# Where four small TensorE jobs stand in a chunked RWKV-7 solve: among the Gram products and the early levels, instead of between the turns of the later levels

## The chip, the core and the metric

The kernel runs on one core of a Trainium2 chip. The metric is the device time of one execution in microseconds (us). The kernel before took 1748.77 us, the median of 3 runs (1746.99 to 1751.68). The engines are called PE (TensorE, matrix products), ACT (ScalarE), DVE (VectorE), POOL (GpSimd) and SP (which only issues transfers).

## The reference, cut to what matters

Two encoder layers on 512 tokens of width 1024. The change lies in the first layer's RWKV-7 mixer, a linear recurrence over time, run forward and backward for 8 heads of width 64:

```
def rwkv7_step(state, inp):
    r, w, k, v, kk, a = inp
    sa = einsum('...vk,...k->...v', state, -kk)
    state = state * w[..., None, :] + sa[..., :, None] * (kk * a)[..., None, :] + v[..., :, None] * k[..., None, :]
    y = einsum('...vk,...k->...v', state, r)
    return state, y
...
decay = exp(-exp(w_log))          # w_log from a low-rank product of wl with w2
a = sigmoid(a0 + low-rank product of al with a2)
bonus = sum(rh[:, :, None] * kh * r_k, axis=(2, 4))
out = (y + bonus[..., None] * vh)
```

The rest (spatial gating, differential attention, cross-attention, gated feed-forward blocks) is not touched.

## The kernel before, in words

The recurrence is solved in chunks of 64 tokens: 8 chunks, 2 directions, and 4 pairs of heads (`j` = 0 to 3, two heads of 64 in 128 partitions). A pair is one call of `pair_pe`, `pair_act`, `pair_dve`, with some work of `pair_pool`. There is no scheduler: each engine runs a list of instructions in the order in which these functions write them, and waits on semaphores. What stands ahead of a waiting instruction on an engine is done, and what stands behind it waits too.

A pair on PE:

- `gram_pe` (L1197): 64x64 products of AR with BET (L1210, into banks 4 and 5 of PSUM), then four groups of 64x128 products (L1224): BET direction 0 into banks 6 and 7, BET direction 1 into banks 0 and 1, KAP direction 0 into 4 and 5, KAP direction 1 into 6 and 7. DVE masks them out of PSUM (`gram_dve`, L1691 to L1699, later `gram_k_dve`, L1705 and L1706).
- Five levels (`lv` = 0 to 4) that double the solved blocks of a triangular inverse. At level 0: products L1333, a mask on DVE (XX, L1745), products L1359, copies on ACT (UU, L1558). At levels 1 to 4: products L1337 for both directions, then the turn of UU for direction 0 (four transposes, L1317, into bank 4), a copy of it on ACT (TT, L1543), the turn for direction 1 into the same bank 4 (so it waits for that copy, `p_t0`), its copy, and the products L1363 in two groups, one for each direction; the second waits for the second copy.
- `side_pe(T, j, s)`, s = 0 to 9: other work put into the levels. An even s = 2 lv stands between the two turns of level lv; an odd s = 2 lv + 1 stands behind the second products of level lv. It holds the bonus product (L1270), the two low-rank halves for the next pair (`lora_pe`, L1193, half 0 and half 1), transposes of AR (s = 5), of BET (s = 6, L1301) and of KAP (s = 7), and the products AXT (s = 8). `side_act` holds ACT's part of each: BON (L1505), the tanh of a half (L1487, TMP), copies AXT, GB (L1522), KPD.
- Steps of the previous pair's chain over chunks (`chain_pe`, L1241 and L1246) stand behind each of the two sides.
- A tail (L1379 to L1419), then the next pair's Gram products.

In the last pair (`j` = 3) gate products (L1261) stand in the place of the low-rank halves; in the first pair turns of values (L1137) stand in the place of chain steps, and ACT also carries copies of another part (HIS, L1088).

A product of float32 operands is two passes in the trace, a transpose is one, so 32 products are x64 there.

Of the kernel before, what the change touches and what calls it, by code (L numbers as in the profile page):

```python
# [29 lines left out]
NT = SEQ // P  # L30
# [60 lines left out]
def build(nc, a, out):  # L91
    sems = {}

    def S(name):
        if name not in sems:
            sems[name] = nc.alloc_semaphore(name)
        return sems[name]
# [1092 lines left out]
    def lora_pe(e, j, which, b0):  # L1190
# [3 lines left out]
                          start=True, stop=True)  # L1194
        mm.then_inc(S("p_lora"), 1)

    def gram_pe(T, j):  # L1197
        e = T.e
        ar = AR[j % 2]
        e.wait_ge(S("p_fm"), j + 1)  # L1200
        e.wait_ge(S("p_bet"), j + 1)
        if j > 0:
            e.wait_ge(S("p_rfree"), j)
        else:
            e.wait_ge(S("sgu_s"), SGU_G)
        for d in range(2):
            for t in range(NT):
                for hh in range(2):
                    for x in range(2):
                        mm = e.matmul(PS[xs(x), 4 + hh, (d * NT + t) * CH:(d * NT + t) * CH + CH],  # L1210
                                      ar[half(hh), d, 0, chunk(t, x)], BET[half(hh), d, chunk(t, x)], start=True, stop=True)
        mm.then_inc(S("p_a"), 1)

        for l, d, b in ((BET, 0, 6), (BET, 1, 0), (KAP, 0, 4), (KAP, 1, 6)):
            if l is KAP:
                e.wait_ge(S("p_afree" if d == 0 else "p_bfree"), 2 * j + (2 if d == 0 else 1))
            elif j > 0:
                e.wait_ge(S("p_yfree" if d == 0 else "p_pfree"), j)
            elif d == 1:
                e.wait_ge(*at("zu", "ev", 4))  # L1220
            for t in range(NT):
                for hh in range(2):
                    for x in range(2):
                        mm = e.matmul(PS[xs(x), b + hh, t * P:t * P + P].rearrange("p (s k) -> p s k", s=2),  # L1224
                                      l[half(hh), d, chunk(t, x)], ar[half(hh), d, 0:2, chunk(t, x)], start=True, stop=True)
            mm.then_inc(S("p_g"), 1)
# [37 lines left out]
    def side_pe(T, j, s):  # L1264

        e = T.e
        if s == 2:
            e.wait_ge(S("p_gfree"), 2 * (j + 1))
            e.wait_ge(S("p_bonus"), j + 1)
            e.matmul(PS[:, 6, :], rk("bones"), TMP[1][:, 0, :], start=True, stop=True).then_inc(S("p_bonmm"), 1)  # L1270
        elif s == 3:
            e.wait_ge(S("p_bonfree"), j + 1)
            if j + 1 < NJ:
                lora_pe(e, j + 1, 0, 6)
            else:
                gates_pe(e, 0)
        elif s == 4:
            if j + 1 < NJ:
                e.wait_ge(S("p_lorafree"), 2 * j + 3)
                lora_pe(e, j + 1, 1, 6)  # L1280
            else:
                e.wait_ge(S("f_gg"), 2)
                e.wait_ge(S("f_bg"), 2)
                gates_pe(e, 2)
        elif s == 5:
            if j + 1 < NJ:
                e.wait_ge(S("p_lorafree"), 2 * j + 4)
            else:
                e.wait_ge(S("f_gg"), NJ)
                e.wait_ge(S("f_bg"), NJ)  # L1290
            for d in range(2):
                for t in range(NT):
                    for hh in range(2):
                        mm = e.transpose(PS[:, 6 + hh, (d * NT + t) * HD:(d * NT + t) * HD + HD],
                                         AR[j % 2][half(hh), d, 0, t * P:t * P + P], KC[half(hh), HD * hh:HD * hh + HD])
            mm.then_inc(S("p_tok"), 1)
        elif s in (6, 7):
            e.wait_ge(S("p_tokfree"), 3 * j + s - 5)
            for d in range(2):
                for t in range(NT):  # L1300
                    mm = e.transpose(PS[:, 6 + d, t * P:t * P + P], (BET, KAP)[s - 6][:, d, t * P:t * P + P], ident)  # L1301
            mm.then_inc(S("p_tok"), 1)
        elif s == 8:
            e.wait_ge(S("p_tokfree"), 3 * j + 3)
            if j == 0:
                e.wait_ge(S("rw0_vtk"), NT)
            for d in range(2):
                for u in range(8):
                    hh, t = divmod(u, NT)
                    for x in range(2):  # L1310
                        mm = e.matmul(PS[xs(x), 6 + d, u * CH:u * CH + CH], GKA[xs(x), d, u, :],
                                      VTK[xs(x), t, j * P + HD * hh:j * P + HD * hh + HD], start=True, stop=True)
                mm.then_inc(S("p_x0"), 1)
# [182 lines left out]

    def side_act(A, j, s):
        e = A.e
        if s == 1 and j + 1 == NJ:
            e.wait_ge(S("p_bonus"), NJ)  # L1500
            fin_square_act(e, 0)
            fin_square_act(e, 1)
        elif s == 2:
            e.wait_ge(S("p_bonmm"), j + 1)
            e.activation(BON[j][:, :], PS[:, 6, :], ACT.Copy).then_inc(S("p_bonfree"), 1)  # L1505
        elif s in (3, 4):
            if j + 1 < NJ:
                prep_tanh_act(e, j + 1, s - 3, 6)
            else:
                fin_gate_act(e, 2 * s - 6)  # L1510
                fin_gate_act(e, 2 * s - 5)
        elif s == 5:
            e.wait_ge(S("p_tok"), 3 * j + 1)
# [4 lines left out]
        elif s in (6, 7):  # L1518
            e.wait_ge(S("p_tok"), 3 * j + s - 4)
            for d in range(2):  # L1520
                if s == 6:
                    i = e.activation(units(GB[:, d, :, CH:P]), PS[:, 6 + d, :].rearrange("p (t b k) -> p b t k", b=2, k=HD),  # L1522
                                     ACT.Copy)
                else:
                    i = e.activation(KPD[:, d, :, :], PS[:, 6 + d, :].rearrange("p (t k) -> p t k", k=P), ACT.Copy)
            i.then_inc(S("p_tokfree"), 1)
            if s == 7 and j + 1 < NJ:
                prep_exp_act(e, j + 1)
            elif s == 7:
                e.wait_ge(S("p_bet"), NJ)  # L1530
                hi_part(A)
        elif s == 9 and j + 1 == NJ:
            e.wait_ge(S("c_yfree"), j * STEPS)
            fin_square_act(e, j - 1)
        elif s == 8:
            for d in range(2):
                e.wait_ge(S("p_x0"), 2 * j + d + 1)
                e.activation(AXT[:, d, :, HD:P], PS[:, 6 + d, :].rearrange("p (u k) -> p u k", k=HD), ACT.Copy)\
                    .then_inc(S("p_ax"), 1)

    def turn_u_act(e, j, lv, d):
        e.wait_ge(S(f"p_tn{d}"), j * (LV - 1) + lv)
        e.activation(TT[:, d, :, :], PS[:, 4, :].rearrange("p (u k) -> p u k", k=CH), ACT.Copy).then_inc(S(f"p_t{d}"), 1)  # L1543

    def pair_act(A, j):
        e = A.e
        for lv in range(LV):
            if lv > 0:
                turn_u_act(e, j, lv, 0)
# [235 lines left out]
    def fin_square_act(e, j):  # L1785
        e.activation(YSQ[j][:, :], YL[:, j, :], ACT.Square).then_inc(S("f_sq"), 1)
# [1082 lines left out]
```

## Time and profile before

| what | value |
|---|---|
| median of 3 runs | 1748.77 us |
| the profiled execution, own time | 1745.65 us |
| its span in the trace | 1743.9 us |
| PE busy | 1690.4 us (97%) |
| DVE, ACT, POOL busy | 1044.2, 815.2, 457.6 us |
| the four pairs: their first Gram products start at | 153.3, 197.8, 245.1, 290.9 us |

The profile's page gives the busy time of each engine, the chain of work that ended last, and groups of instructions by line. A busy PE is not a PE at its peak: ends of products are modelled, and one that waits for its turn inside the array counts as busy. In the chain, "issue" is time in which an engine waited for nothing that the profile shows. Brackets in a row of the timeline give the engine's idle time ahead of that row and what ended it.

### The profile page before, as it was taken

How to read it: one execution, taken by the hardware profiler on the slowest of the kernel's cores; microseconds unless marked ns; L12 is line 12 of the kernel's file. 1: busy time of each engine (PE TensorE's matmuls, PEld its weight loads, DVE VectorE, ACT ScalarE, POOL GpSimd, SP SyncE). 2: the span in 40 equal slices, each digit the busy share in tenths (PEclk: the TensorE clock that was granted, in tenths of full speed). 3: DMA queues.
4: the chain of work that ended last, by engine and by line, in shares of the span. 5: the costliest groups of instructions: out<-in, count | busy, mean ns of one | idle time of the engine just before them, and what ended most of it. 6: DMA issues, size and time to landing. Idle time of an engine off the chain costs nothing.

```text
span 1743.9 us, 29667 instructions
## 1 busy us (share of the span) xinstructions
PE 1690.4 (97%) x12773; PEld 1385.1 (79%) x12773; DVE 1044.2 (60%) x1308; ACT 815.2 (47%) x1237; POOL 457.6 (26%) x407
## 2 busy tenths in 40 slices
PE   7999899899999999999999999999999999999999
PEld 6878788778888787888887886668887788788887
DVE  5478677356343666766675455975434455685667
ACT  5254555536553433543355236865654343453344
POOL 2002322220100472245310220540010166114620
PEclk9999999999999999999999999999999999999999
DMA  7210000243222565365443222003431275356534
GB/s 255 85 48 2 4 5 6 73 169 123 95 97 73 202 233 181 126 245 183 163 169 108 97 75 71 1 2 121 145 108 41 94 264 196 132 195 239 196 102 155
DMA packets 116925, 212.70 MB, mean 122 GB/s; under 512 B 4247, under 2 KB 50938, under 8 KB 116794
## 3 DMA queue, kind: packets, MB, share of 16 engines
q1 hardware_dynamic: 103239, 159.59, 27.2%
q0 software_dynamic: 13264, 51.09, 8.2%
q8 instruction: 101, 1.65, 0.4%
q14 instruction: 30, 0.25, 0.0%
q10 hardware_dynamic: 291, 0.12, 0.0%
HBM read 185.62 MB, written 25.17 MB: 121 GB/s over the span
## 4 chain that ended last, share of the span: by engine, by line
PE 74%; DVE 11%; ACT 6%; issue 3%; POOL 3%; DMA 3%; SPq 0%; DVEq 0%; ACTq 0%; POOLq 0%
PE PS L431 50%; PE PS L538 10%; POOL DW L671 2%; DVE WLO L397 1%; ACT WHI L386 1%; PE PS L1929 1%; DVE SS L2237 1%; PE PS L1898 1%; DMA WRAW<-ab_w_in 1%; PE PS L937 1%; DMA diff_dn<-DW 1%; PE PS L1379 1%; DVE AT L2249 1%; DVE SQN L1013 1%; PE PS L2068 1%
## 5 line engine op out<-in xcount | busy, mean ns | idle before, releaser
L397 DVE TENSOR_TENSOR WLO<-WRAW,WHI 128x2048 fp32r<-128x2048 f32 (+1 forms) x106 | 249.1, 2361 | 296.0 <-ACT WHI L386 296.0
L431 PE MATMUL PS<-HIS,WHI 128*128 128x512 f32 x856 | 334.6, 391 | 4.8 <-DVE LOS L2412 2.1
L431 PE MATMUL PS<-LOS,WHI 128*128 128x512 f32 x856 | 333.1, 389 | 0.0
L431 PE MATMUL PS<-HIS,WLO 128*128 128x512 f32 x856 | 333.1, 389 | 0.0
L386 ACT ACTIVATE WHI<-WRAW 128x2048 fp32r<-128x2048 f32 (+1 forms) x107 | 203.0, 1907 | 229.0 <-PE PS L431 181.6
L431 PE MATMUL PS<-WHI,HIS 128*128 128x512 f32 x608 | 240.4, 395 | 1.1 <-DVE LOS L728 1.1
L431 PE MATMUL PS<-WLO,HIS 128*128 128x512 f32 x608 | 236.9, 390 | 0.0
L431 PE MATMUL PS<-WHI,LOS 128*128 128x512 f32 x608 | 236.7, 389 | 0.0
L431 PEld LDWEIGHTS PS<-HIS,WHI 128*128 128x128 f32 x856 | 160.7, 188 | 42.4 <-issue 5.7
L431 PEld LDWEIGHTS PS<-HIS,WLO 128*128 128x128 f32 x856 | 160.7, 188 | 33.5
L431 PEld LDWEIGHTS PS<-LOS,WHI 128*128 128x128 f32 x856 | 160.7, 188 | 32.9
L431 PEld LDWEIGHTS PS<-WHI,HIS 128*128 128x128 f32 x608 | 114.2, 188 | 26.3 <-issue 1.8
L431 PEld LDWEIGHTS PS<-WLO,HIS 128*128 128x128 f32 x608 | 114.1, 188 | 24.3
L431 PEld LDWEIGHTS PS<-WHI,LOS 128*128 128x128 f32 x608 | 114.2, 188 | 22.9 <-issue 0.2
L538 PE MATMUL PS<-WHI,SHI 128*128 128x512 f32 x308 | 120.1, 390 | 0.8 <-DVE SLO L554 0.8
L538 PE MATMUL PS<-WLO,SHI 128*128 128x512 f32 x308 | 119.8, 389 | 0.0
L538 PE MATMUL PS<-WHI,SLO 128*128 128x512 f32 x308 | 119.8, 389 | 0.0
L394 DVE TENSOR_TENSOR WLO<-PW,WHI 128x1536 fp32r<-128x1536 f32 (+1 forms) x56 | 92.4, 1650 | 26.1 <-ACT WHI L382 25.9
L382 ACT ACTIVATE WHI<-PW 128x1536 fp32r<-128x1536 f32 (+1 forms) x56 | 76.8, 1378 | 64.2 <-PE PS L538 54.8
L671 POOL TENSOR_TENSOR DW<-RW 128x512 f32<-128x512 f32 x44 | 88.6, 2031 | 61.8 <-DMA diff_dn<-DW 46.1
L2024 ACT ACTIVATE SHI<-GX 128x256 fp32r<-128x256 f32 x44 | 18.4, 418 | 149.9 <-POOL GX L624 94.7
L746 POOL TENSOR_TENSOR SM<-SM 128x1 f32<-128x1 f32 x16 | 12.2, 797 | 244.8 <-DVE SM L754 236.4
(327 smaller groups left out, 2844.3 us busy)
## 6 DMA issues: line engine op xcount, KB each, us to landing
WRAW<-ffn_w_up SPq DMA_DIRECT2D x88, 512.0 KB, 4.9
RW<-ffn_w_down POOLq DMA_DIRECT2D x22, 1024.0 KB, 7.3
diff_dn<-DW POOLq DMA_DIRECT2D x22, 1024.0 KB, 5.3
WRAW<-cross_wkv SPq DMA_DIRECT2D x16, 1024.0 KB, 5.0
PW<-diff_dn SPq DMA_DIRECT2D x8, 1536.0 KB, 9.3
WRAW<-diff_w_in SPq DMA_DIRECT2D x12, 1024.0 KB, 5.1
WRAW<-ab_w_in SPq DMA_DIRECT2D x10, 1024.0 KB, 5.7
PW<-diff_dn SPq DMA_DIRECT2D x8, 1280.0 KB, 7.5
```

The lines of the kernel that those rows point to most:

```text
L382: A.e.activation(WHI[place(i)][:, 0:a1 - a0, :], PW[PW_PLACE[q]][:, a0:a1, :], ACT.Copy)\
L386: A.e.activation(part(WHI[place(i)], i), part(WRAW[raw_slot[i]], i), ACT.Copy).then_inc(S("w_hi"), 1)
L394: V.e.tensor_tensor(WLO[place(i)][:, 0:a1 - a0, :], PW[PW_PLACE[q]][:, a0:a1, :], WHI[place(i)][:, 0:a1 - a0, :].bitcast(F32), ALU.subtrac ...
L397: V.e.tensor_tensor(part(WLO[place(i)], i), part(WRAW[raw_slot[i]], i), part(WHI[place(i)], i).bitcast(F32), ALU.subtract).then_inc(S("w_l ...
L431: mm = e.matmul(o, l, r, start=(si == 0 and kk == 0 and q == 0), stop=(si == len(steps) - 1 and kk == nk - 1 and q == 2))
L538: mm = e.matmul(PS[:, bank + t, :], ht[part_of][:, m, t * P:t * P + P], wt[place(i)][:, m - a0, :], start=(fresh and m == 0 and r == 0), s ...
L671: e.tensor_tensor(DW[:, to, :], x, y, ALU.subtract).then_inc(sem(name, "wdif"), 1)
L937: mm = e.transpose(PS[:, bank0 + k % 4, t * P:t * P + P], tok[:, t, k * P:k * P + P], ident)
L1013: V.mine(e.reciprocal(SQN[j][:, :], SQN[j][:, :]))
L1379: mm = e.matmul(PS[xs(x), 2 * d + u // 4, (u % 4) * P:(u % 4) * P + P], UU[xs(x), d, u, :], AXT[xs(x), d, u, :], start=True, stop=True)
L1898: mm = e.matmul(PS[:, 4 * (t % 2) + h // 2, (h % 2) * MEM:(h % 2) * MEM + MEM], QFT[:, 2 * h + k, t * P:t * P + P], KFT[:, 2 * h + k, :], ...
L2024: A.e.activation(SHI[b - 2][:, gi, :], GX[:, (0, 4)[b - 2], gi, :], ACT.Copy).then_inc(sem(name, "hi"), 1)
```

## The change

Four jobs are moved; none is added or taken away.

- BET's transposes leave s = 6 (between the turns of level 3) and stand between BET's two groups of Gram products, in banks 2 and 3. ACT's copy of them (GB) is a new `gram_act`, ahead of level 0.
- The next pair's low-rank half 0 leaves s = 3 and stands between KAP's two groups of Gram products, in banks 2 and 3, behind that copy. Its tanh follows the copy in `gram_act`.
- The bonus product leaves s = 2 (between the turns of level 1) and stands behind level 0 (s = 1), in bank 3.
- The low-rank half 1 leaves s = 4 (between the turns of level 2) and stands at s = 3, where half 0 stood.

```
+    def tokens_pe(e, l, b0):
+        for d in range(2):
+            for t in range(NT):
+                mm = e.transpose(PS[:, b0 + d, t * P:t * P + P], l[:, d, t * P:t * P + P], ident)
+        mm.then_inc(S("p_tok"), 1)
...
         for l, d, b in ((BET, 0, 6), (BET, 1, 0), (KAP, 0, 4), (KAP, 1, 6)):
+            if l is BET and d == 1:
+                if j > 0:
+                    e.wait_ge(S("p_qfree"), j)
+                else:
+                    e.wait_ge(*at("zu", "ev", 4))
+                tokens_pe(e, BET, 2)
+            if l is KAP and d == 1 and j + 1 < NJ:
+                e.wait_ge(S("p_tokfree"), 3 * j + 1)
+                lora_pe(e, j + 1, 0, 2)
...
-        if s == 2:
+        if s == 1:
+            e.wait_ge(S("p_bonus"), j + 1)
+            e.matmul(PS[:, 3, :], rk("bones"), TMP[1][:, 0, :], start=True, stop=True).then_inc(S("p_bonmm"), 1)
+        elif s == 3:
             e.wait_ge(S("p_gfree"), 2 * (j + 1))
...
             if j + 1 < NJ:
-                lora_pe(e, j + 1, 0, 6)
+                lora_pe(e, j + 1, 1, 6)
...
-                if lv == 0 and d == 1 and j > 0:
-                    e.wait_ge(S("p_qfree"), j)
+                if lv == 1 and d == 1:
+                    e.wait_ge(S("p_bonfree"), j + 1)
+                if lv == 0 and d == 1:
+                    if j + 1 < NJ:
+                        e.wait_ge(S("p_lorafree"), 2 * j + 3)
+                    else:
+                        e.wait_ge(S("p_tokfree"), 3 * j + 1)
...
+    def gram_act(e, j):
+        e.wait_ge(S("p_tok"), 3 * j + 1)
+        for d in range(2):
+            i = e.activation(units(GB[:, d, :, CH:P]), PS[:, 2 + d, :].rearrange("p (t b k) -> p b t k", b=2, k=HD), ACT.Copy)
+        i.then_inc(S("p_tokfree"), 1)
+        if j + 1 < NJ:
+            prep_tanh_act(e, j + 1, 0, 2)
+
     def pair_act(A, j):
         e = A.e
+        gram_act(e, j)
```

PE's list at the Gram products of pair 1, before (AR_118 is this pair's AR, U_98 is U0; the brackets name the semaphores waited for):

```order
L1224 MATMUL PS<-AR_118,BET 64x128 [waits p_yfree]
L1224 MATMUL PS<-AR_118,BET 64x128 x15
L1224 MATMUL PS<-AR_118,BET 64x128 [waits p_pfree]
L1224 MATMUL PS<-AR_118,BET 64x128 x15
L1224 MATMUL PS<-AR_118,KAP 64x128 [waits p_afree]
L1224 MATMUL PS<-AR_118,KAP 64x128 x15
L1224 MATMUL PS<-AR_118,KAP 64x128 [waits p_bfree]
L1224 MATMUL PS<-AR_118,KAP 64x128 x15
L1333 MATMUL PS<-U_98,AI 64x64 [waits p_bfree,p_u0]
```

And the same place now (L1237 are the products of L1224, L1344 those of L1333; KC holds the identity):

```order
L1237 MATMUL PS<-AR_118,BET 64x128 [waits p_yfree]
L1237 MATMUL PS<-AR_118,BET 64x128 x15
L1200 MATMUL PS<-KC,BET 128x128 [waits p_qfree]
L1200 MATMUL PS<-KC,BET 128x128 x7
L1237 MATMUL PS<-AR_118,BET 64x128 [waits p_pfree]
L1237 MATMUL PS<-AR_118,BET 64x128 x15
L1237 MATMUL PS<-AR_118,KAP 64x128 [waits p_afree]
L1237 MATMUL PS<-AR_118,KAP 64x128 x15
L1193 MATMUL PS<-ZS_88,WL_73 128x512 [waits p_tokfree]
L1193 MATMUL PS<-ZS_88,WL_73 128x512
L1237 MATMUL PS<-AR_118,KAP 64x128 [waits p_bfree]
L1237 MATMUL PS<-AR_118,KAP 64x128 x15
```

Eight transposes and two low-rank products now stand inside the Gram products, and the first of the low-rank products waits for ACT's copy of the transposes.

ACT's list at levels 2 and 3 of pair 1, before (TMP_114 is the tanh of half 1, UU the copies behind L1363):

```order
L1543 ACTIVATE TT<-PS 128x512 [waits p_tn0]
L1487 ACTIVATE TMP_114<-PS,SM 128x512 [waits p_lora,p_bonmm,p_fm]
L1487 ACTIVATE TMP_114<-PS,SM 128x512
L1543 ACTIVATE TT<-PS 128x512 [waits p_tn1]
L1561 ACTIVATE UU<-PS 128x2x4x64 [waits p_un0]
L1561 ACTIVATE UU<-PS 128x2x4x64 [waits p_un1]
L1515 ACTIVATE AXT<-PS 128x8x64 [waits p_tok]
L1515 ACTIVATE AXT<-PS 128x8x64
L1543 ACTIVATE TT<-PS 128x512 [waits p_tn0]
L1522 ACTIVATE GB<-PS 128x8x64 [waits p_tok]
L1522 ACTIVATE GB<-PS 128x8x64
L1543 ACTIVATE TT<-PS 128x512 [waits p_tn1]
```

And the same place now (L1549 are the copies of L1543, L1576 those of L1561):

```order
L1549 ACTIVATE TT<-PS 128x512 [waits p_tn0]
L1549 ACTIVATE TT<-PS 128x512 [waits p_tn1]
L1576 ACTIVATE UU<-PS 128x2x4x64 [waits p_un0]
L1576 ACTIVATE UU<-PS 128x2x4x64 [waits p_un1]
L1525 ACTIVATE AXT<-PS 128x8x64 [waits p_tok]
L1525 ACTIVATE AXT<-PS 128x8x64
L1549 ACTIVATE TT<-PS 128x512 [waits p_tn0]
L1549 ACTIVATE TT<-PS 128x512 [waits p_tn1]
```

The two copies of a level's turns now follow each other with nothing between them, at level 2 and at level 3.

## Rows read from the trace of the kernel before

**Rows 1.** Busy time over the four pairs (length, then each engine's us and instructions)

```profile
150.00:340.00 190.00, 173.28 (x5630) 150.62 (x5628) 130.30 (x204) 99.57 (x164) 50.65 (x38) 1.00 0.07 21
```

**Rows 2.** Chain of waits, Gram stages of pairs 1, 2, 3 (start us, us, what)

```profile
198.27 1.80 issue
...
203.31 0.49 issue
...
211.15 0.52 issue
...
243.62 1.36 issue
...
247.97 0.84 issue
...
292.06 0.83 PE PS L1224 x30
292.89 1.37 issue
```

**Rows 3.** DMA queues from 150 to 340 us (packets, MB, share of 16 engines)

```profile
q8 instruction: 44, 0.72, 1.6%
```

**Rows 4.** Chain of waits, the moved kinds of work between other products

```profile
214.94 1.06 PE PS L1193 x4
...
228.01 1.04 PE PS L1301 x8
...
306.50 1.91 PE PS L1261 x4
```

**Rows 5.** Timeline of PE in pair 2 (start us, us, engine, line)

```profile
248.99 2.01 PE L1224 MATMUL PS<-AR,KAP 64*64 64x128 f32 x63
250.76 2.14 PE L1333 MATMUL PS<-U,AI 64*64 64x64 f32 x64
252.71 2.13 PE L1359 MATMUL PS<-XX,TT 64*64 64x64 f32 x64
254.88 0.45 PE L1241 MATMUL PS<-QT,PT 64*64 64x64 f32 x8
...
256.68 0.66 PE L1317 MATMUL PS<-KC,UU 128*128 128x128 f32 x4
...
258.03 0.65 PE L1317 MATMUL PS<-KC,UU 128*128 128x128 f32 x4
...
260.16 1.13 PE L1193 MATMUL PS<-ZS,WL 64*128 64x512 f32 x4
...
262.76 0.65 PE L1317 MATMUL PS<-KC,UU 128*128 128x128 f32 x4
...
264.41 0.66 PE L1317 MATMUL PS<-KC,UU 128*128 128x128 f32 x4
...
267.13 0.71 PE L1294 MATMUL PS<-KC,AR 64*128 64x64 f32 x16
...
270.08 0.66 PE L1317 MATMUL PS<-KC,UU 128*128 128x128 f32 x4
...
271.44 0.64 PE L1317 MATMUL PS<-KC,UU 128*128 128x128 f32 x4
...
273.99 1.09 PE L1301 MATMUL PS<-KC,KAP 128*128 128x128 f32 x8
```

**Rows 6.** Timeline of ACT in pair 2

```profile
253.90 0.60 ACT L1558 ACTIVATE UU<-PS 128x512 f32<-128x512 f32 x1 [7.45 <-PE PS L1359]
...
257.37 0.60 ACT L1543 ACTIVATE TT<-PS 128x512 f32<-128x512 f32 x1 [1.89 <-PE PS L1317]
...
264.60 1.26 ACT L1487 ACTIVATE TMP<-PS,SM 128x512 f32<-128x512 f32 x2 [0.56 <-PE PS L1193]
...
271.64 1.09 ACT L1522 ACTIVATE GB<-PS 128x512 f32<-128x512 f32 x2 [0.28 <-PE PS L1301]
```

**Rows 7.** Timeline of PE in pair 0

```profile
158.40 2.08 PE L1333 MATMUL PS<-U,AI 64*64 64x64 f32 x64 [0.20 <-DVE GB L1696]
```

More of the change, by code:

```diff
@@ L1266, in side_pe @@
         e = T.e
-        if s == 2:
+        if s == 1:
+            e.wait_ge(S("p_bonus"), j + 1)
+            e.matmul(PS[:, 3, :], rk("bones"), TMP[1][:, 0, :], start=True, stop=True).then_inc(S("p_bonmm"), 1)
+        elif s == 3:
             e.wait_ge(S("p_gfree"), 2 * (j + 1))
[L1269 to L1272, printed above, removed]
             if j + 1 < NJ:
-                lora_pe(e, j + 1, 0, 6)
+                lora_pe(e, j + 1, 1, 6)
             else:
@@ L1277, in side_pe @@
         elif s == 4:
[L1278 to L1281, printed above, removed]
+            if j + 1 == NJ:
                 e.wait_ge(S("f_gg"), 2)
@@ L1296, in side_pe @@
             mm.then_inc(S("p_tok"), 1)
[L1297 to L1302, printed above, removed]
+        elif s == 7:
+            e.wait_ge(S("p_tokfree"), 3 * j + 2)
+            tokens_pe(e, KAP, 6)
         elif s == 8:
@@ L1498, in side_act @@
         e = A.e
[L1499 to L1503, printed above, removed]
+        if s == 1:
             e.wait_ge(S("p_bonmm"), j + 1)
-            e.activation(BON[j][:, :], PS[:, 6, :], ACT.Copy).then_inc(S("p_bonfree"), 1)
+            e.activation(BON[j][:, :], PS[:, 3, :], ACT.Copy).then_inc(S("p_bonfree"), 1)
+            if j + 1 == NJ:
+                fin_square_act(e, 0)
+                fin_square_act(e, 1)
         elif s in (3, 4):
-            if j + 1 < NJ:
-                prep_tanh_act(e, j + 1, s - 3, 6)
-            else:
+            if s == 3 and j + 1 < NJ:
+                prep_tanh_act(e, j + 1, 1, 6)
+            elif j + 1 == NJ:
                 fin_gate_act(e, 2 * s - 6)
@@ L1512, in side_act @@
         elif s == 5:
-            e.wait_ge(S("p_tok"), 3 * j + 1)
+            e.wait_ge(S("p_tok"), 3 * j + 2)
             for d in range(2):
@@ L1517, in side_act @@
             i.then_inc(S("p_tokfree"), 1)
-        elif s in (6, 7):
-            e.wait_ge(S("p_tok"), 3 * j + s - 4)
+        elif s == 7:
+            e.wait_ge(S("p_tok"), 3 * j + 3)
             for d in range(2):
[L1521 to L1525, printed above, removed]
+                i = e.activation(KPD[:, d, :, :], PS[:, 6 + d, :].rearrange("p (t k) -> p t k", k=P), ACT.Copy)
             i.then_inc(S("p_tokfree"), 1)
-            if s == 7 and j + 1 < NJ:
+            if j + 1 < NJ:
                 prep_exp_act(e, j + 1)
-            elif s == 7:
+            else:
                 e.wait_ge(S("p_bet"), NJ)
@@ L1543, in turn_u_act @@
         e.activation(TT[:, d, :, :], PS[:, 4, :].rearrange("p (u k) -> p u k", k=CH), ACT.Copy).then_inc(S(f"p_t{d}"), 1)
+    def gram_act(e, j):
[3 more added lines that the diff above has]
+        i.then_inc(S("p_tokfree"), 1)
+        if j + 1 < NJ:
+            prep_tanh_act(e, j + 1, 0, 2)
     def pair_act(A, j):
         e = A.e
+        gram_act(e, j)
         for lv in range(LV):
```

2 lines of the change are left out of this document (removed).

## The prediction

> **What bounds the kernel now.** I read the windows of the four pairs first, then the chain of waits through them, then the timelines of PE and ACT at the places that the change touches. In the windows the reader is to see that PE is busy for 173.28 of 190.00 us [rows 1]: no other engine is near that, so the stage ends when PE's list ends, and an edit is worth what it does to the time between two starts on PE. The other engines matter only where PE waits for them.
>
> In the chain the reader is to see two kinds of wait. One is "issue", time for which the profile names no other engine: six such gaps, 0.49 to 1.80 us long, at or near the Gram products of pairs 1 to 3 [rows 2]. In the same 190 us the instruction queue moved 44 packets while PE ran 5630 passes [rows 1, 3], which is one packet for 128 passes (a weight load and a product each). So I take the gaps for waits for code: a block of 128 passes can't start before its packet has come, and short products (L1333: 64 passes from 250.76 to 252.71, 30 ns each [rows 5]) run through a block in less than the 4.3 us that a packet took on average (190.00 by 44). The other kind is ACT's copy TT between and behind the two turns of a level.
>
> In the timeline of PE the distances from start to start tell what a place costs. At level 1 the second turn starts 1.35 us after the first (256.68 to 258.03), and that is the copy and not the bonus product between them: ACT's TT runs from 257.37 to 257.97 [rows 5, 6]. At level 2 the distance is 1.65 (262.76 to 264.41), set by the low-rank half; at level 3 it is 1.36 (270.08 to 271.44), the copy again.
>
> **The change part by part.** Terms are taken for a pair, start to start on PE, and then added over the pairs. Positive is slower.
>
> *What the Gram stage and level 0 gain in work.* The eight transposes cost 1.04 between 64x64 products, the low-rank half 1.06, and the bonus product 0.95 (half of the 1.91 of the two gate products, which are of the same shape and stand between the same kinds of work) [rows 4]. Together 3.05 in pairs 0 to 2. Pair 3 has no low-rank half: 1.99.
>
> *What hides it there.* Where PE runs without a wait, L1333 starts 0.24 before the modelled end of L1224 (250.76 against 248.99 + 2.01 = 251.00) [rows 5]; so each gap that the views show is 0.24 longer from start to start. In pair 1 the transposes fall into the block that ends in the 0.49 gap, among KAP's groups, which gives back 0.73; the 0.52 gap at 211.15 stands behind all three jobs and gives back 0.76 [rows 2]. In pair 2 the 0.84 gap (1.08) comes between BET and KAP, which runs from 248.99, so it stands behind the transposes and gives them back whole; the chain step at 254.88 waited for the mask GKR behind L1359's end at 254.84 (0.04, so 0.28), which the bonus product now covers [rows 2, 5]. The gaps at 198.27 and 243.62 stand ahead of the moved work and stay. In pair 3 the 1.37 gap at 292.89 comes after 30 of the 32 passes of BET's first group, so just ahead of the transposes, and gives nothing back [rows 2]. In pair 0 there is no gap of this kind, but L1333 waited 0.20 for DVE (0.44) [rows 7], and GKR held the next step as in pair 2, 0.28. For pair 3 I take the same two, 0.72.
>
> Left over: pair 0, 3.05 - 0.72 = 2.33. Pair 1, 3.05 - 1.49 = 1.56. Pair 2, 3.05 - 1.36 = 1.69. Pair 3, 1.99 - 0.72 = 1.27.
>
> *What the levels give back.* Level 1: nothing. The bonus product stood in the 1.35 that the copy takes in any case, and half 1 takes the place of half 0 behind it. Level 2: the second turn comes at 1.35 instead of 1.65, 0.30. From the second turn to the next work behind both groups of L1363 it takes 2.13 at level 1 (258.03 to 260.16), where nothing waits, and 2.72 at level 2 (264.41 to 267.13), where ACT's tanh (264.60, 1.26) stands ahead of the second copy: 0.59. Level 3: 0.01 between the turns, and 2.55 (271.44 to 273.99) against 2.13 behind them, where GB's copy (1.09) stood in the way: 0.42 [rows 5, 6]. So 1.32 in pairs 1 and 2. Pair 3 keeps its gate products between the turns of level 2 and gains level 3 alone, 0.43. In pair 0 ACT also carries the HIS copies in these levels, which the change does not move; bounds 0 and 1.32, and I take half, 0.66, since neither is nearer.
>
> *New waits.* The transposes wait for QT's copies, which ACT makes while PE runs L1210; the half waits for GB's copy, 1.09 on an ACT that stood idle for 7.45 there [rows 6], and BET's second and KAP's first group stand between (32 passes each; 63 took 2.01 [rows 5]), so I count nothing. If ACT were late, KAP's second group and all behind it would be late by as much. L1333's second group waits for the tanh, 1.26 on ACT against 32 passes of KAP and 32 of L1333. L1337's second group at level 1 waits for BON's copy, with a chain step and the first group ahead of it. POOL's L1650 writes BET for the next pair and waits for the transposes; it can only start earlier, and the next pair's L1210 needs it much later, so I count nothing. No transfer is moved.
>
> *The sum.* Pair 0: 2.33 - 0.66 = 1.67. Pair 1: 1.56 - 1.32 = 0.24. Pair 2: 1.69 - 1.32 = 0.37. Pair 3: 1.27 - 0.43 = 0.84. Together 3.1 us slower: 1745.65 + 3.1 = 1748.8 by the profiled execution. That execution lies 3.1 below the median of the runs, so the forecast of a median is 1748.77 + 3.1 = 1751.9, 0.18% more. I call anything within 0.3% (5.2 us) no change, which is about what a measurement of this kernel can tell.
>
> **The rivals.**
>
> *The levels don't give it back (slower).* The place is XX's mask on DVE at level 3 and the code block that ends there: if the second group of L1363 then waits for one of these instead of for ACT's copy, the 0.66 + 1.32 + 1.32 + 0.43 = 3.73 of the levels go, and the sum is 6.8: 1755.6. It decides for "slower" once less than 1.6 of the 3.73 comes. For it: DVE has its scans at level 2, just ahead of that mask. Against it: the rows name ACT, not DVE, at both places, and ACT's obstacle is gone.
>
> *The gaps don't fill (slower).* If the "issue" gaps are not bound to the count of passes, work put ahead of them only pushes them back: 0.73 + 0.76 + 1.08 = 2.6 more, 5.7 in all, 1754.4. For it: the profile names no releaser there. Against it: the packets and the 128 passes. The Trainium skill, "Runtime: NRT & Kernel Launch", section "Instruction fetch mechanics", says that a queue of the sequencer's own fills a buffer of 2048 instructions for this engine in blocks of 256, and that the cost of crossing a block is mostly hidden; by that the gaps would have another cause and this rival would hold. The trace agrees with the blocks (44 packets for 5630 passes of two instructions) and not with the hiding.
>
> *All of it hides (no change, a little faster).* If the moved work costs nothing in the Gram stage, because DVE's masks or the code set its pace from end to end, only the 3.73 remains: 1745.0. For it: six gaps there. Against it: three of them stand ahead of the moved work.
>
> *It also lets the code run ahead (faster).* If slow passes in a block let later packets come early, the 1.80 and 1.36 gaps at 198.27 and 243.62 go as well: 1741.9. Against it: a whole tail of short products stands between the moved work and the next pair's Gram products.
>
> **How the numbers follow.** Forecast 0.50; levels don't give back 0.18; gaps don't fill 0.12; all hides 0.14; code runs ahead 0.06. So slower 0.30, same 0.64 (0.50 + 0.14), faster 0.06. The forecast's own bounds: the three jobs' prices by a tenth each way (0.3 in a pair, 1.1 in all), pair 0's levels by 0.66 each way, pair 3's two small waits by 0.72 upwards: 1751.9 less 1.8 and more 2.5. The range reaches over both slower cases and leaves out the two below: 1747.5 to 1756.5.
>
> **What would show it.** In the profile after, at pair 2: the first and second turns of levels 2 and 3 both 1.35 apart; the second group of L1363 there no longer behind ACT; no "issue" gap between the transposes and L1333's successor in pairs 1 and 2, but those at the tail's end and ahead of the transposes unchanged; the chain step of level 1 later by some 1.5 to 2.3 us from the pair's start, and level 4 by less than half of that. Wrong would be the forecast if the Gram stage got no longer, or if the wait at level 3 came back under another engine's name. By this the span would be near 1747.0 (1743.9 + 3.1); one under 1743 or over 1752 would show the size wrong.

## The result: slower by 0.4%, near the upper end of the range

| | median of the runs | runs | against before |
|---|---|---|---|
| before | 1749.36 us (1744.34 to 1751.68) | 6 | |
| after | 1755.41 us (1752.93 to 1759.53) | 6 | 1.0042, 95% interval 1.0024 to 1.006 |

The medians lie 6.0 us apart where 3.1 were forecast: inside the range of 1747.5 to 1756.5, but slower, not "no change". The page of the kernel after, its busy times:

```profile
PE 1698.3 (97%) x12773; PEld 1390.6 (79%) x12773; DVE 1046.0 (60%) x1308; ACT 816.8 (46%) x1237; POOL 458.2 (26%) x407
```

DVE, ACT and POOL are busy within 1.8 us of before; PE is busy 7.9 us longer. Part of that is the clock: the profiled execution (own time 1759.53, span 1757.7) ran at a mean granted clock of 0.996, that of before at 1.000. Windows of after (length, busy us of PE, PEld, DVE, ACT, POOL with instructions, granted clock, DMA share, GB/s):

```profile
150.00:340.00 190.00, 170.23 (x5316) 146.02 (x5316) 127.45 (x198) 97.99 (x161) 48.47 (x36) 0.98 0.06 17
...
190.00:194.00 4.00, 4.00 (x70) 4.00 (x66) 4.00 (x9) 0.87 (x3) 0.21 (x1) 0.58 0.02 4
194.00:251.00 57.00, 49.59 (x1738) 43.53 (x1734) 37.73 (x60) 26.00 (x41) 15.56 (x13) 1.00 0.02 4
251.00:255.00 4.00, 3.97 (x105) 3.64 (x106) 1.62 (x3) 1.09 (x2) 1.72 (x2) 0.57 0.01 4
255.00:340.00 85.00, 77.62 (x2443) 66.15 (x2442) 54.32 (x92) 44.81 (x74) 18.72 (x14) 1.00 0.11 33
```

In the same 190 us PE gets through 5316 passes, not 5630, and is idle 19.8 us, not 16.7 [rows 1]. Two short stretches stand at 0.58 and 0.57, that is mostly at 1.2 GHz instead of 2.4. (More such time lies behind the pairs: from 356 to 360 us the clock is 0.65.) What follows compares starts on PE stage by stage, so that these stretches can be told from the rest.

The chain of waits, its "issue" gaps at the Gram stages after (start us, us, what):

```profile
201.38 1.80 issue
...
249.12 1.91 issue
```

The gaps of 0.49, 0.52 and 0.84 [rows 2] are gone, and those ahead of the moved work stay, as forecast (1.80 is 1.80 again, 1.36 is 1.91 in this execution). At level 3 of pair 1 the chain before ran over ACT's GB copy:

```profile
225.60 1.08 ACT GB L1522 x2
226.68 0.50 ACT TT L1543
```

After, it runs over a scan on DVE:

```profile
226.19 1.23 DVE TMP L1609
227.41 3.23 DVE TMP L1610
230.64 0.18 DVE QT L1267
230.82 0.21 DVE YL L1270
231.03 0.04 issue
231.07 0.45 PE PS L1254 x8
```

Two engines' timelines show why (L1609 and L1610 are the two scans of the next pair's decay, L1665 is POOL's product of the rate and KK into the next pair's BET, L1303 AR's transposes, L1323 a turn, L1254 the chain step behind it, L1200 KAP's transposes; brackets: idle time ahead and what ended it):

```profile
222.41 1.05 POOL L1660 TENSOR_SCALAR TMP<-TMP 128x1024 f32<-128x1024 f32 x1 [6.08 <-ACT TMP L1498]
226.77 2.79 POOL L1665 TENSOR_TENSOR BET<-KK,TMP 128x1024 f32<-128x1024 f32 x1 [3.32 <-PE PS L1303]
...
226.19 1.23 DVE L1609 TENSOR_TENSOR_SCAN TMP<-RC,TMP 128x512 f32<-128x512 f32 x1
227.33 3.31 DVE L1610 TENSOR_TENSOR_SCAN TMP<-RC,TMP 128x512 f32<-128x512 f32 x1
...
277.12 3.32 DVE L1610 TENSOR_TENSOR_SCAN TMP<-RC,TMP 128x512 f32<-128x512 f32 x1
...
223.74 0.66 PE L1323 MATMUL PS<-KC,UU 128*128 128x128 f32 x4 [0.69 <-ACT TT L1549]
...
225.88 0.71 PE L1303 MATMUL PS<-KC,AR 64*128 64x64 f32 x16
...
229.41 0.66 PE L1323 MATMUL PS<-KC,UU 128*128 128x128 f32 x4 [0.69 <-ACT TT L1549]
231.07 0.45 PE L1254 MATMUL PS<-QT,PT 64*64 64x64 f32 x8 [1.01 <-DVE YL L1270]
...
232.90 1.09 PE L1200 MATMUL PS<-KC,KAP 128*128 128x128 f32 x8
```

The second scan takes 3.31 us where the first takes 1.23. It ends at 230.64, 1.08 after POOL's product (226.77 + 2.79 = 229.56): it has waited for POOL and then run. The chain step on PE waits for DVE's steps behind that scan. Second turn to KAP's transposes is 3.49 (229.41 to 232.90) where 2.13 was forecast. Pair 2's scan at 277.12 takes as long, and the same distance is 2.90 there. In the kernel before the scans were over when POOL began:

```profile
222.31 1.23 DVE L1594 TENSOR_TENSOR_SCAN TMP<-RC,TMP 128x512 f32<-128x512 f32 x1
223.45 1.20 DVE L1595 TENSOR_TENSOR_SCAN TMP<-RC,TMP 128x512 f32<-128x512 f32 x1
...
227.09 1.56 DVE L1606 TENSOR_SCALAR TMP<-TMP,COLS,SM 128x1024 f32<-128x1024 f32 x1
...
225.74 2.37 POOL L1650 TENSOR_TENSOR BET<-KK,TMP 128x1024 f32<-128x1024 f32 x1 [4.01 <-PE PS L1301]
```

There it lay over another DVE instruction, the scaling L1606, which takes 1.56 under it (0.81 after, at L1621, where POOL stands idle), and the chain above does not run over that.

The reason is a line that the diff does not touch. POOL's product waits for the second of the pair's three signals `p_tok`. Before, the second was BET's transposes, at level 3; now BET's come first, and the second is AR's, at the end of level 2. So the product starts earlier in its pair, 25.91 us behind pair 1's Gram start (226.77 less 200.86) where it was 27.99 before (225.74 less 197.75). Before, it came 1.09 after the end of the second scan; now it comes 0.56 ahead of that scan's start. Its operand is ready at 223.46 (222.41 + 1.05): released by BET's own signal it could run ahead of both scans.

### The profile page after: what moved, and what is told of

Read it like the earlier page. It is cut to its first block, busy times and chain, and to the rows that moved or that the text cites. A ratio compares the mean times of both kernels' runs of the same rounds, so it can differ in the third digit from the quotient of the medians.

```text
span 1757.7 us, 29668 instructions
## 1 busy us (share of the span) xinstructions
PE 1698.3 (97%) x12773; PEld 1390.6 (79%) x12773; DVE 1046.0 (60%) x1308; ACT 816.8 (46%) x1237; POOL 458.2 (26%) x407
## 4 chain that ended last, share of the span: by engine, by line
PE 74%; DVE 11%; ACT 6%; issue 3%; POOL 3%; DMA 3%; SPq 0%; DVEq 0%; ACTq 0%; POOLq 0%
PE PS L431 49%; PE PS L538 10%; POOL DW L671 2%; DVE WLO L397 1%; ACT WHI L386 1%; PE PS L1944 1%; DVE SS L2252 1%; PE PS L1913 1%; DMA WRAW<-ab_w_in 1%; PE PS L937 1%; PE PS L1237 1%; PE PS L1390 1%; DMA diff_dn<-DW 1%; DVE AT L2264 1%; DVE SQN L1013 1%
## 5 line engine op out<-in xcount | busy, mean ns | idle before, releaser
L431 PE MATMUL PS<-HIS,WHI 128*128 128x512 f32 x856 | 334.5, 391 | 4.5 <-DVE LOS L2427 1.5
L431 PE MATMUL PS<-HIS,WLO 128*128 128x512 f32 x856 | 333.2, 389 | 0.0
L431 PE MATMUL PS<-LOS,WHI 128*128 128x512 f32 x856 | 333.1, 389 | 0.0
L431 PE MATMUL PS<-WHI,HIS 128*128 128x512 f32 x608 | 241.5, 397 | 1.1 <-DVE LOS L728 1.1
L431 PE MATMUL PS<-WHI,LOS 128*128 128x512 f32 x608 | 237.6, 391 | 0.0
L431 PE MATMUL PS<-WLO,HIS 128*128 128x512 f32 x608 | 237.6, 391 | 0.0
L431 PEld LDWEIGHTS PS<-HIS,WHI 128*128 128x128 f32 x856 | 160.7, 188 | 42.6 <-issue 3.6
L431 PEld LDWEIGHTS PS<-HIS,WLO 128*128 128x128 f32 x856 | 160.7, 188 | 33.7
L431 PEld LDWEIGHTS PS<-LOS,WHI 128*128 128x128 f32 x856 | 160.7, 188 | 32.5
L431 PEld LDWEIGHTS PS<-WHI,HIS 128*128 128x128 f32 x608 | 114.8, 189 | 26.5 <-issue 1.8
L431 PEld LDWEIGHTS PS<-WLO,HIS 128*128 128x128 f32 x608 | 114.7, 189 | 24.4
L431 PEld LDWEIGHTS PS<-WHI,LOS 128*128 128x128 f32 x608 | 114.8, 189 | 23.2 <-issue 0.2
```

The lines of the kernel that those rows point to most:

```text
L431: mm = e.matmul(o, l, r, start=(si == 0 and kk == 0 and q == 0), stop=(si == len(steps) - 1 and kk == nk - 1 and q == 2))
```

## The bill by stages

Starts on PE, after less before, and the forecast's terms sorted into the same stages (the 0.52 gap of pair 1 lay 13.4 us behind its Gram start, so in the second row). "Early" is the first experiment below. Each column is one profiled execution.

| stage | forecast | after | early |
|---|---|---|---|
| Gram start to L1333's products: pairs 0, 1, 2, 3 | 1.66, 1.37, 1.02, 0.60 | 1.75, 1.75, 2.79, 0.70 | 1.75, 1.48, 1.22, 0.98 |
| to level 1's second turn | 0.67, 0.19, 0.67, 0.67 | 0.75, 0.05, 0.59, 0.89 | 0.75, 0.05, 0.59, 0.89 |
| to level 3's first turn | -0.45, -0.89, -0.89, 0 | -0.40, -0.87, -1.06, 0 | -0.39, -0.88, -0.90, 0 |
| to the tail | -0.21, -0.43, -0.43, -0.43 | 0.10, 0.91, 0.33, -0.44 | -0.10, -0.35, -0.44, -0.44 |
| sum to the tails | 3.1 | 7.8 | 4.2 |
| tail to the next Gram start | 0 | 1.15, 1.10, -0.20 | 1.32, 0.28, 0.07 |

Two stages of after are off. Level 3 of pairs 1 and 2 costs 1.34 and 0.76 more than forecast: the scan. Pair 2's Gram stage costs 1.57 more than in "early", and it holds the stretch at half clock that starts behind 251; pair 0's tail holds the other. Pair 1's tail is 1.10 longer, of which 0.55 is the gap of 1.36 that is 1.91 here.

Such gaps differ from one execution to another with PE's list unchanged. In "before, with two copies split" below, where nothing is moved on PE, the 0.49, 0.52 and 0.84 are 0.20, 0.14 and 0.56. A difference of half a microsecond in one stage of one profile can be that alone.

## The experiments

The mean granted clock differs a little from run to run, and the last column takes that out: the time of each run less that of the kernel before at the same clock, from the runs of before that were measured with it (1.23 us for each 0.001 of clock, a line through 70 runs of the kernel before in three sets); mean and standard error. For the kernel after, whose line is that of all 70, it is +7.5; the three sets differ by up to 1.4 us at equal clock, so this figure is the least sure. The column is not what a run takes: if a kernel brings on a low clock itself, that cost is left out of it. The medians have it in.

| kernel | median us | ratio to before, 95% | at equal clock, us |
|---|---|---|---|
| product early | 1753.27 | 1.0032 (1.0020 to 1.0043) | +5.0, 0.3 |
| product late | 1754.24 | 1.0038 (1.0023 to 1.0052) | +5.1, 0.4 |
| bonus back | 1753.18 | 1.0034 (1.0021 to 1.0048) | +4.2, 0.3 |
| BET's transposes back | 1751.77 | 1.0021 (1.0008 to 1.0033) | +3.6, 0.5 |
| early, and bonus back | 1751.27 | 1.0012 (1.0000 to 1.0025) | +1.9, 0.3 |
| BET's transposes alone, product early | 1752.62 | 1.0027 (1.0014 to 1.0040) | +3.4, 0.5 |
| the same, product late | 1748.11 | 1.0017 (1.0001 to 1.0033) | +0.9, 0.4 |
| low-rank halves alone | 1746.75 | 0.9992 (0.9982 to 1.0002) | +0.1, 0.2 |
| before, with two copies split | 1747.67 | 0.9986 (0.9975 to 0.9996) | -3.0, 0.5 |
| low-rank halves, GB's copy split | 1747.39 | 1.0000 (0.9986 to 1.0014) | 0.0, 0.4 |

**POOL's product off the scan, early.** The kernel after, with the wait set to BET's own signal:

```diff
-            e.wait_ge(S("p_tok"), 3 * j - 1)
+            e.wait_ge(S("p_tok"), 3 * j - 2)
             e.tensor_tensor(BET[:, :, :], both(KK[:, j, :]), TMP[1][:, :, :], ALU.mult).then_inc(S("p_bk"), 1)
```

> The changed kernel, with POOL's product of KK and the rate (it writes the next pair's BET) waiting for the first p_tok signal of the pair, BET's transposes, instead of the second, which is AR's transposes in the new order. Theory A, collision: in the changed kernel this product (226.77 to 229.56) lies over DVE's second scan, which takes 3.31 instead of 1.2 us, and level 3's mask comes late. Then here the scans take 1.2 each in pairs 1 and 2, the distance from the second turn of level 3 to KAP's transposes falls from 3.5 (pair 1) and 2.9 (pair 2) to about 2.1, and the time falls by 1.5 to 2.2: a ratio to before near 1.003. Theory B, the clock alone (four stretches at half clock in the changed kernel's profile): the ratio stays near 1.004 whenever such stretches are there, and the level keeps its distances. Theory C, the Gram stage's terms alone: nothing changes.

Its timeline at level 3 of pair 1:

```profile
223.03 2.37 POOL L1665 TENSOR_TENSOR BET<-KK,TMP 128x1024 f32<-128x1024 f32 x1
...
225.97 1.23 DVE L1609 TENSOR_TENSOR_SCAN TMP<-RC,TMP 128x512 f32<-128x512 f32 x1
227.12 1.20 DVE L1610 TENSOR_TENSOR_SCAN TMP<-RC,TMP 128x512 f32<-128x512 f32 x1
...
228.90 0.66 PE L1323 MATMUL PS<-KC,UU 128*128 128x128 f32 x4 [0.69 <-ACT TT L1549]
...
231.03 1.09 PE L1200 MATMUL PS<-KC,KAP 128*128 128x128 f32 x8
```

The scan is back at 1.20 and the step at 2.13 (228.90 to 231.03), the forecast's number. The time falls by 2.1 from median to median, or 2.5 at equal clock. Against the runs of before that go with each, the medians give less, 6.0 down to 5.1, and the two ratios' intervals overlap; two more pairs of kernels below differ by this overlap, and at equal clock by 2.3 and 2.5. The rows are as theory A said. Early's profile has a stretch at half clock too (0.58, shown below), and level 3 is short all the same, so the clock alone (theory B) is not what lengthened it.

**The same from the other side, late.** `3 * j - 1` becomes `3 * j`, KAP's signal.

> The changed kernel, with POOL's product for the next pair's BET held back until KAP's transposes are done (third signal of the pair, not the second). Theory (what costs is that POOL's product lies over DVE's second scan): the scan at level 3 takes 1.2 us again, as it does when the product starts early, and the step from level 3's second turn to KAP's transposes is back near 2.1 us, in pairs 1 and 2 alike; the product then lies under DVE's scaling of the next pair's rows instead; time 1752.5 to 1754.5. Rival (the product must come early; what hurts is its lateness, not the overlap): pairs 1 and 2 stay as long as in the changed kernel or get longer, 1755 or more.

```profile
225.62 1.23 DVE L1609 TENSOR_TENSOR_SCAN TMP<-RC,TMP 128x512 f32<-128x512 f32 x1
226.77 1.20 DVE L1610 TENSOR_TENSOR_SCAN TMP<-RC,TMP 128x512 f32<-128x512 f32 x1
...
232.25 2.62 POOL L1665 TENSOR_TENSOR BET<-KK,TMP 128x1024 f32<-128x1024 f32 x1 [9.36 <-PE PS L1200]
...
228.85 0.66 PE L1323 MATMUL PS<-KC,UU 128*128 128x128 f32 x4 [0.69 <-ACT TT L1549]
...
230.98 1.09 PE L1200 MATMUL PS<-KC,KAP 128*128 128x128 f32 x8
```

5.5 us later than POOL had it, and again 1.20 and 2.13. So it is the overlap and not the lateness. The product lies beside other DVE instructions here. The masks among them, which read PSUM, take as long as elsewhere (XX, two in 1.29); an instruction on SBUF operands at its end, L1637, takes 1.17 for 0.68, and the step above is not longer for it. The medians alone would not tell this kernel from the one after; the rows and the equal-clock column do.

**The bonus product back** between level 1's turns (`if s == 1:` to `if s == 2:`, bank 3 to 6, with its waits), and this together with the early product:

> The changed kernel with the bonus product back between the turns of level 1. By the sum of the prediction the bonus cost 0.95 less 0.28 behind level 0 in each pair and nothing between the turns: 2.7 us less than the changed kernel, a ratio to before near 1.0025. Collision theory: the same, and level 3 stays as long as in the changed kernel. Rival, the bonus product was hidden behind level 0 by the mask GKR: no difference, ratio 1.004.

> The changed kernel, with POOL's product released early and the bonus product back between the turns of level 1. Theory: the two add, since the one lies at level 3 and the other at level 0: the early product takes away what it did alone (2 to 2.6 us) and the bonus what it did alone (1.3 to 3.5), which leaves +0.5 to +3 over the kernel before, with the same-clock runs at 1748 to 1750.5. Rival (both only shift PE against the same packets of code, and don't add): 1752 to 1753.5, as each alone.

At equal clock 3.3 less than after in the one case, 3.1 less than "early" in the other; 1.0 and 2.0 by the medians, each against its own runs of before. The overlap is worth 2.3 between these two kernels at equal clock (4.2 to 1.9) and 2.5 between after and "early", so at equal clock the two effects add. Level 3 of the first kernel stays long, with scans of 3.32 and 3.31, as the collision theory said. By starts on PE the stage up to level 1's second turn is 0.78, 0.92, 0.93 and 0.92 shorter than in after, 3.6 in all: nearly the product's whole 0.95 in each pair, and not 0.95 less 0.28. (The stage table's 2.28 is lower because before has its 0.52 gap in that stage of pair 1.)

**BET's transposes back** at level 3, with GB's copy:

```diff
-                tokens_pe(e, BET, 2)
...
-        elif s == 7:
+        elif s in (6, 7):
...
+            tokens_pe(e, (BET, KAP)[s - 6], 6)
```

> The changed kernel with BET's transposes and their copy back at level 3; the low-rank halves and the bonus stay moved. By the prediction's terms the transposes cost 1.04 less 0.44, 0.73, 1.08, 0.44 in the Gram stages of pairs 0 to 3 and gave back some 0.2 to 0.43 at level 3: together near nothing, so the time stays within 1 us of the changed kernel. Collision theory: p_tok's second signal is BET's again, POOL's product no longer meets the scan, and the time falls by 1.5 to 2. Issue gaps inside KAP's groups come back in pairs 1 and 2 if they are waits for code.

3.9 less than after at equal clock, 2.4 by the medians, each against its own runs of before: more than either side of its expectation. POOL's product comes after the scans again, which take 1.2, and gaps come back among the Gram products, 0.65 in pair 1 and 0.84 in pair 2, as was to be seen if they are waits for code. This undoes both the transposes' cost and the order of the signals, so alone it does not say which. The next two do.

**BET's transposes alone**, in the kernel before, with POOL's product early, and then late:

```diff
+                tokens_pe(e, BET, 2)
...
-            e.wait_ge(S("p_tok"), 3 * j - 1)
+            e.wait_ge(S("p_tok"), 3 * j - 2)
```

> The kernel before, with BET's transposes and their copy alone moved among the Gram products, and POOL's product released by their signal (so early). Theory (each job costs its passes less the gap for code that it fills, and gives back what its copy held up): 1.04 a pair, less 0.44 in pair 0, 0.73 in pair 1, 1.08 in pair 2 and up to 0.72 in pair 3, less 0.42 a pair at level 3: +0.2, -0.1, -0.5 and -0.1 to +0.6; time within 1 us of before. Rival (the Gram stage costs more than the sum of the jobs says): +1.5 to +3, above all in pairs 0 and 3.

> As the kernel with BET's transposes and copy alone moved, but POOL's product held back until KAP's transposes are done. Theory (the moved transposes cost what the terms say, +0.2, -0.1, -0.5 and up to +0.6; all the rest of that kernel's 4.5 us was the scan under POOL's product): the first scan at level 3 takes 1.2 us instead of 3.26, the second turn of level 3 to KAP's transposes 2.1 instead of 4.5, and the time is within 1.5 us of before. Rival (transposes in the Gram stage themselves cost 3 or more): 1751 or more, with the scans at 1.2 all the same.

The first of them came out at +3.4 (4.5 by the medians), and neither side of its expectation had the reason. With the low-rank halves in their old places the rate is ready later in the pair than in "early" (the product's operand comes from POOL at 220.34), and the product, though released early, falls onto the first scan; the longest steps are in pairs 1 and 2, not in 0 and 3. Its rows at level 3 of pair 1 (L1660 is the product here, L1324 the turn, L1251 the chain step):

```profile
219.29 1.05 POOL L1655 TENSOR_SCALAR TMP<-TMP 128x1024 f32<-128x1024 f32 x1 [8.37 <-ACT TMP L1494]
220.43 2.67 POOL L1660 TENSOR_TENSOR BET<-KK,TMP 128x1024 f32<-128x1024 f32 x1
...
220.93 3.26 DVE L1604 TENSOR_TENSOR_SCAN TMP<-RC,TMP 128x512 f32<-128x512 f32 x1
...
224.00 0.65 PE L1324 MATMUL PS<-KC,UU 128*128 128x128 f32 x4 [0.69 <-ACT TT L1546]
225.73 0.69 PE L1251 MATMUL PS<-QT,PT 64*64 64x64 f32 x8 [1.08 <-DVE YL L1267]
...
228.48 1.39 PE L1200 MATMUL PS<-KC,KAP 128*128 128x128 f32 x8
```

Its clock just there (a window of PE, PEld, DVE, ACT, POOL, granted clock, as above):

```profile
226.00:228.00 2.00, 2.00 (x72) 2.00 (x74) 1.98 (x5) 0.22 (x1) 0.00 (x0) 0.50 0.00 0
```

And with the product late:

```profile
221.30 1.23 DVE L1604 TENSOR_TENSOR_SCAN TMP<-RC,TMP 128x512 f32<-128x512 f32 x1
...
227.77 2.62 POOL L1660 TENSOR_TENSOR BET<-KK,TMP 128x1024 f32<-128x1024 f32 x1 [7.05 <-PE PS L1200]
...
224.37 0.65 PE L1324 MATMUL PS<-KC,UU 128*128 128x128 f32 x4 [0.69 <-ACT TT L1546]
...
226.50 1.09 PE L1200 MATMUL PS<-KC,KAP 128*128 128x128 f32 x8
```

One wait alone takes 2.5 us off at equal clock (4.5 between the medians, 1.4 of which lies between the two sets of before's runs beside them, 1748.13 and 1746.70), and the step goes from 4.48 to 2.13. Not all of that step is the scan. In this execution PE ran at half clock in it (0.50 from 226 to 228, 1.00 at that place with the product late), and the same products took 0.69 and 1.39 where they take 0.45 and 1.09 in after. Whether the wait for the scan brought the clock down isn't shown: in after PE waited 1.01 at the same place and kept it. The eight transposes themselves cost 0.9 over four pairs at equal clock; the terms that the expectation gives for them were right within about 1. By starts on PE, pair 1's and pair 2's Gram stages are 0.26 and 0.01 longer for 1.04 of work, as they should be if the transposes fill the gaps there.

**The low-rank halves alone**, in the kernel before:

```diff
+            if l is KAP and d == 1 and j + 1 < NJ:
+                lora_pe(e, j + 1, 0, 2)
...
-                lora_pe(e, j + 1, 0, 6)
+                lora_pe(e, j + 1, 1, 6)
```

> The kernel before, with the two low-rank halves alone moved (half 0 among the Gram products, half 1 behind level 1's products). Theory: 1.06 in pairs 0 to 2, less 0.44 in pair 0 and 0.76 in pair 1, less 0.89 at level 2 in pairs 1 and 2 (half of it in pair 0): +0.2, -0.6, +0.2, and nothing in pair 3: within 1 us of before. Rival (the levels give nothing back by this alone): +2.

+0.1 (1.4 faster by the medians, an interval that includes no change), as the theory said: level 2 pays for the Gram stage.

**Level 2's and 3's gain without moving anything on PE.** The kernel before, with ACT's two copies of the tanh of half 1 and of GB split, one ahead of the second turn's copy, one behind it:

```diff
+            elif s == 6: gb_act(e, 0)
...
                 turn_u_act(e, j, lv, 1)
+            if lv == 2 and j + 1 < NJ:
+                tanh_act(e, j + 1, 1, 6, 1)
+            elif lv == 3:
+                gb_act(e, 1)
```

> The kernel before, with ACT's order alone changed: at level 2 the tanh of half 1, at level 3 the copy GB, are split, one direction ahead of the copy TT of the second turn and one behind it. If ACT's copies in front of TT were what the second group of L1363 waited for (0.59 at level 2, 0.42 at level 3), these waits go without anything being moved on PE: 0.5 to 0.9 less in each of pairs 0 to 2, 0.4 in pair 3, 2 to 3 us faster than before, ratio 0.9985. If the level's time is taken back by the wait for code or by DVE's mask: no change.

ACT at level 3 of pair 2 in it (L1556 are the turns' copies; compare GB and its neighbours in [rows 6]):

```profile
267.81 0.60 ACT L1496 ACTIVATE GB<-PS 128x512 f32<-128x512 f32 x1 [0.28 <-PE PS L1301]
268.31 0.59 ACT L1556 ACTIVATE TT<-PS 128x512 f32<-128x512 f32 x1
268.79 0.61 ACT L1496 ACTIVATE GB<-PS 128x512 f32<-128x512 f32 x1
```

The second turn's copy starts 0.50 behind the start of GB's first half; in before it stood behind both, which take 1.09. From level 1's second turn to the tail the pairs are 0.23, 1.01, 0.73 and 0.45 shorter than before's, 2.4 together, where 2 to 3 was expected. This is the one kernel that is faster than both before and after, by 0.14% (0.04 to 0.25); the medians lie only 0.5 us apart, and at equal clock the difference is 3.0.

**Half of each.** The low-rank halves alone, with GB's copy split:

> The kernel with the low-rank halves alone moved, and ACT's GB copy at level 3 split, one direction ahead of the second turn's copy and one behind it. Expected: it keeps level 2's gain and gives back at level 3 what the split gave before (0.42 a pair, 1.3 to 1.7 in all): 1 to 2 us faster than the low-rank halves alone, 1744.5 to 1746. Rival (POOL's product or DVE is the next to end there): no faster than the low-rank halves alone.

1.0000 (0.9986 to 1.0014): the expected 1 to 2 us did not show in the time. By starts on PE its four pairs are 1.9 us shorter than before's from Gram start to tail, so the split does its part there. In the profiled execution the gain is lost again right behind the pairs. The first of PE's long products (L431) there starts 2.70 us earlier than in before, and a group of products some 25 us further on (L1459, L1453 in before) 0.30 later, with a stretch at half clock between them that before's profile hasn't. The window from 344 to 348, here and then in before:

```profile
344.00:348.00 4.00, 4.00 (x24) 3.29 (x25) 0.67 (x3) 0.00 (x0) 3.59 (x1) 0.50 0.00 0
```

```profile
344.00:348.00 4.00, 4.00 (x42) 3.76 (x43) 0.67 (x3) 0.00 (x0) 1.26 (x1) 1.00 0.01 4
```

The profiles of "two copies split" (0.50 in this window) and of "transposes alone, product late" (0.55) have the same loss, 2.9 and 3.9 us between the same two places. It does not go with short pairs alone: after has such a stretch too, a little later. Why the other executions show no gain at equal clock stays open, since only one of them has a trace.

## Why the prediction was wrong

The failed step is in "New waits": "POOL's L1650 writes BET for the next pair and waits for the transposes; it can only start earlier, and the next pair's L1210 needs it much later, so I count nothing." The wait is for a count, not for the transposes, and the change altered which transposes that count stands for. POOL's product did start earlier in its pair, as the sentence says (25.91 us for 27.99), but that was no reason for nothing: I asked only who needs POOL's result, not beside what it runs. Where a POOL product lies over a scan on DVE, the later of the two waits: 3.31 and 3.32 us for 1.20. That put 2.1 us by the stage table (2.5 at equal clock) on a term that the sum has at nothing. The prediction's own sign of being wrong came true, "if the wait at level 3 came back under another engine's name": it is DVE's.

It is not the whole miss. With the overlap taken away, "early" is still 5.1 us slower by the medians (5.0 at equal clock), at the edge of the 5.2 that I had called no change, where 3.1 was forecast: the terms for the bonus product and for pairs 0 and 3 were too small, as listed below.

The Trainium skill, "SBUF — State Buffer", section "Who interferes with whom", says that the port pair which DVE and GpSimd share is "an exclusive lock", and that a DVE instruction with two SBUF inputs contends with a GpSimd instruction that reads SBUF. The trace agrees: the blocked scan ends 1.08 us after POOL's product does (229.56 to 230.64), and 1.09 in the kernel with BET's transposes alone (223.10 to 224.19), as if it had waited for the whole product and then run its 1.2, and not merely been slowed. I did not bring that rule in.

Point by point:

- *Pace set by PE, prices of the jobs:* right for the transposes and the halves. The bonus product was put at 0.67 a pair (0.95 less the 0.28 of the mask GKR that it was to cover); moving it alone measures 0.78 to 0.93, so little or nothing of the 0.28 came.
- *Gaps fill:* right in the main. 0.49, 0.52 and 0.84 are gone, the two ahead of the moved work stay, and with BET's transposes put back 0.65 and 0.84 return. But a gap's length is not a fixed price (0.49 was 0.20 in another execution), and the count of six left out one of 1.21 at 289.19, ahead of pair 3's Gram products; the sum does not use it. The rival "gaps don't fill" forecast a figure near the result (1754.4), but its mechanism is not what is seen. That the gaps are waits for code stays an inference from counts; one more count agrees with it, the 128 passes in before between the gaps at 243.62 and 247.97 (6 of L1419, 64 of L1210, 58 of L1224).
- *Levels give back:* level 2 right (0.87 and 1.06 for 0.89). In pairs 1 and 2 the second turn follows the first by 1.34 to 1.35 at levels 1 to 3. Level 3 would have given 0.35 and 0.44 for 0.43, as "early" shows, and lost 0.91 and 0.33 instead. That is the form of the first rival (1755.6: "DVE has its scans at level 2"), and its place was right; but it forecast that the gain would be missing at all levels, and named no part for POOL. That its figure lies 0.2 us from the measured median is luck.
- *Terms too small:* pair 0 by 0.3 and pair 3 by 0.6 in "early", 0.9 together. In pair 0 level 3 gave 0.10 for 0.21 (ACT's HIS copies stay there; that they are the reason was not tested); in pair 3 the Gram stage has 0.98 for 0.60 and the bonus product 0.89 for 0.67.
- *The sum:* 3.1 forecast, 4.2 in "early" to the tails. For the overlap the stage table says 1.34 + 0.76 = 2.1 and the equal-clock column 2.5. That makes 6.3 to 6.7, beside 6.0 by medians and 7.5 at equal clock.
- *The clock* was nowhere in the forecast. It explains the last line of the stage table for pair 0: 1.15 and 1.32 in after and "early", which have a stretch at half clock in that tail, and -0.17 in "bonus back", which has none (8.98 us against before's 9.15). What brings it isn't settled. PE had been busy alike ahead of that place, in "early" (first) and in "bonus back" (second; windows as above), and the clock fell in the one and not in the other:

```profile
186.00:190.00 4.00, 2.30 (x83) 1.89 (x82) 3.97 (x4) 3.96 (x7) 2.35 (x1) 1.00 0.00 2
190.00:194.00 4.00, 4.00 (x62) 4.00 (x55) 4.00 (x9) 0.87 (x2) 0.01 (x1) 0.58 0.01 4
```

```profile
186.00:190.00 4.00, 2.29 (x87) 1.89 (x85) 3.96 (x4) 3.85 (x7) 2.36 (x1) 1.00 0.00 2
190.00:194.00 4.00, 4.00 (x115) 4.00 (x108) 4.00 (x9) 1.90 (x3) 0.00 (x0) 1.00 0.02 4
```

  Between runs at equal clock the difference is no smaller than between the medians, and the one run of after with a mean clock of 1.000 took 1752.93 us where before's profiled run, also at 1.000, took 1745.65. So the clock is not what made the change slower.

## What to carry to other kernels

When a job that signals a counting semaphore is moved past another that signals the same one, every wait on that count now means another event: list the waiters on all engines, also those whose lines the diff leaves alone. For a POOL instruction that moves, ask not only who needs its result but what DVE runs beside it, and place it in a stretch where DVE reads PSUM (the masks took 1.29 under POOL's product as without it) or stands idle. Where a copy on a third engine delays a chain, splitting the copy around the chain's own can be cheaper than moving its work: here 0.14% faster, where moving the low-rank halves was worth nothing (+0.1 us at equal clock) and moving BET's transposes cost 0.9. And a gain in one stage can be lost in the next: look at the granted clock behind it before the stage's figure is taken for the kernel's.

## What was not expected of the hardware

- The price of a scan that starts under a POOL product is most of the product: 2.1 us of 2.79 (3.31, 3.32 and 3.26 for 1.2). A TENSOR_SCALAR of 128x1024 on DVE waits too: 1.43 beside POOL's rate in before's level 2, 0.69 in after, where POOL stands idle then.
- A mean granted clock lower by 0.001 goes with 1.2 us more of 1746, and the 70 runs of the kernel before differ by up to 0.006 in it. By that, as an estimate, a difference of 0.2% between two medians of six runs can be the clock alone.
